# The order of the 256-column matmuls inside projection and output-projection tiles of a fused two-block transformer kernel

## The reference

```python
def memory_cross_attention(h, mem_n, w_cq, w_ck, w_cv, w_co):
    q = (h @ w_cq).reshape(bsz, seqlen, CROSS_HEADS, CROSS_HEAD_DIM)
    k = (mem_n @ w_ck).reshape(bsz, mlen, CROSS_HEADS, CROSS_HEAD_DIM)
    v = (mem_n @ w_cv).reshape(bsz, mlen, CROSS_HEADS, CROSS_HEAD_DIM)
    ...
    return o @ w_co

x = x + hybrid_mixer(rms_norm(x, norm_mix_w[l]), w_in_mix[l], ...)
x = x + memory_cross_attention(rms_norm(x, norm_cross_w[l]), rms_norm(mem, norm_mem_w[l]), ...)
```

## Time and profile before

| | |
|---|---|
| median of 3 runs | 1856.13 us |
| the profiled execution, its own time | 1856.43 us |
| its span, first to last instruction | 1854.6 us |
| TensorE matmuls, busy | 1839.3 us (99%), 12202 matmuls |
| TensorE weight loads, busy | 1657.6 us (89%), 12202 |
| VectorE | 1292.1 us (70%) |
| ScalarE | 968.9 us (52%) |
| GpSimd | 133.5 us (7%) |
| granted TensorE clock | 0.998, tenths 9 in all 40 slices |

### The profile page before, as it was taken

How to read it: one execution, slowest core, us unless ns; L and a number is a source line. 1 busy time by engine, 2 the same in 40 slices (tenths; PEclk the granted TensorE clock), 3 DMA queues, 4 the chain that set the end, 5 groups by cost and what they waited for, 6 DMA issues and landing times.

```text
span 1854.6 us, 29790 instructions
## 1 busy us (share of the span) xinstructions
PE 1839.3 (99%) x12202; PEld 1657.6 (89%) x12202; DVE 1292.1 (70%) x1499; ACT 968.9 (52%) x1329; POOL 133.5 (7%) x166
## 2 busy tenths in 40 slices
PE   9999999999999999999999999999999999999998
PEld 7888999899998888888899988888889969998887
DVE  7875687776567765776685777567758786467763
ACT  6654465565445554554454555455544575355542
POOL 1200000131010001000120100000000001010000
PEclk9999999999999999999999999999999999999999
DMA  7555454434435554555454455555554505435553
GB/s 289 212 204 182 160 174 156 149 127 169 159 132 204 187 190 174 208 191 191 159 182 154 165 187 198 184 184 197 186 192 175 199 10 193 160 119 211 185 201 113
DMA packets 45725, 325.15 MB, mean 175 GB/s; under 512 B 5293, under 2 KB 5429, under 8 KB 6560
## 3 DMA queue, kind: packets, MB, share of 16 engines
q1 hardware_dynamic: 44208, 316.56, 47.7%
q0 software_dynamic: 1248, 6.77, 1.1%
q10 hardware_dynamic: 144, 0.00, 0.0%
HBM read 322.26 MB, written 1.06 MB: 174 GB/s over the span
## 4 chain that ended last, share of the span: by engine, by line
PE 93%; DVE 5%; ACT 1%; issue 1%; POOL 0%; DMA 0%; POOLq 0%; DVEq 0%; SPq 0%; ACTq 0%
PE PS L688 25%; PE PS L747 13%; PE PS L691 13%; PE PS L561 9%; PE PS L562 9%; PE PS L563 9%; PE PS L749 6%; DVE w_lo L2082 1%; DVE xT L2105 1%; PE PS L799 1%; PE PS L781 1%; PE PS L1300 1%; PE PS L1339 1%; PE PS L1319 1%; ACT w_hi L1396 0%
## 5 line engine op out<-in xcount | busy, mean ns | idle before, releaser
L2082 DVE TENSOR_TENSOR w_lo<-raw,w_hi 128x2048 fp32r<-128x2048 f32 x295 | 679.0, 2304 | 261.6 <-ACT w_hi L1396 261.4
L688 PE MATMUL PS<-xT,w_hi 128*128 128x512 f32 x2096 | 732.0, 395 | 1.7 <-DVE arena L2244 1.5
L1396 ACT ACTIVATE w_hi<-raw 128x2048 fp32r<-128x2048 f32 x295 | 562.9, 1908 | 194.5 <-PE PS L563 143.7
L691 PE MATMUL PS<-xT,w_lo 128*128 128x256 f32 x2096 | 582.3, 278 | 0.0
L688 PEld LDWEIGHTS PS<-xT,w_hi 128*128 128x128 f32 x2096 | 393.2, 188 | 94.2 <-DVE arena L2244 1.8
L691 PEld LDWEIGHTS PS<-xT,w_lo 128*128 128x128 f32 x2096 | 394.0, 188 | 0.2
L561 PE MATMUL PS<-xT,w_hi 128*128 128x256 f32 x592 | 170.6, 288 | 0.5 <-DVE w_lo L2082 0.3
L747 PE MATMUL PS<-more_hidden,w_hi 128*128 128x512 f32 x480 | 169.6, 395 | 0.0
L562 PE MATMUL PS<-xT,w_hi 128*128 128x256 f32 x592 | 167.4, 283 | 0.0
L563 PE MATMUL PS<-xT,w_lo 128*128 128x256 f32 x592 | 167.4, 283 | 0.0
L747 PE MATMUL PS<-mT,w_hi 128*128 128x512 f32 x384 | 136.1, 395 | 0.0
(11 more groups left out here) (352 smaller groups left out, 3112.2 us busy)
## 6 DMA issues: line engine op xcount, KB each, us to landing
raw<-weights SPq DMA_DIRECT2D x299, 1024.0 KB, 4.8
arena<-mems POOLq DMA_DIRECT2D x5, 1024.0 KB, 5.1
x<-x_in SPq DMA_DIRECT2D x1, 1024.0 KB, 7.1
out<-x SPq DMA_DIRECT2D x4, 256.0 KB, 2.9
both<-toep POOLq DMA_DIRECT2D x1, 512.0 KB, 4.0
arena<-toep POOLq DMA_DIRECT2D x1, 512.0 KB, 4.5
con<-consts SPq DMA_DIRECT2D x1, 498.0 KB, 13.1
arena<-dtw SPq DMA_DIRECT2D x1, 256.0 KB, 13.5
```

Source lines behind the costliest of these rows:

```text
L688: pe.matmul(PS[:, bank + part, :], w_hi[:, slot, w:w + P], xT[:, k].rearrange("p a b -> p (a b)"), start=k == 0, stop=False, skip_group_ch ...
L691: last = pe.matmul(PS[:, bank + part, 0:S], w_lo[:, slot, w:w + P], xT_hi[:, k, :], start=False, stop=k == KC - 1, skip_group_check=True)
L1396: act.activation(w_hi[:, slot, :], raw[:, raw_slot, :], ACT.Copy).then_inc(hi_ready, 1)
L2082: dve.tensor_tensor(w_lo[:, slot, :], raw[:, raw_slot, :], w_hi[:, slot, :], ALU.subtract).then_inc(lo_ready, 1)
```

## The change

In `proj` the two halves of the output now run side by side: for each `k`, for each of the three products, one matmul into part 0 and one into part 1. In `accumulate` two chunks `d` run side by side in the same way, for each row chunk and product one matmul into each of the two. The number of matmuls, their shapes and their sums stay as they were (in tiles with `rows_out` the second and third product change places). `mid` and `mid2` fall after the same number of matmuls as before, 24 and 36. In a fresh tile there is now a wait before every `k`, each followed by 6 matmuls. In the last accumulate tile both waits for `x_ready` stand ahead of the pair, and both `chunk_done` come at its end.

```diff
-                for part, first in ((0, 0), (0, 4), (1, 0), (1, 4)) if fresh is None else ((0, 0), (1, 0), (0, 4), (1, 4)):
-                    for k in range(first, first + 4):
-                        if fresh is not None and part == 0:
-                            pe.wait_ge(split_done, fresh * KC + k + 1)
...
-                        last = mm3(o, a, b, c, d, k == 0 and (part == 0 or fresh is None), k == KC - 1)
+                for k in range(KC):
+                    if fresh is not None:
+                        pe.wait_ge(split_done, fresh * KC + k + 1)
+                    for product in range(3):
+                        for part in range(2):
+                            if rows_out:
+                                a = (hi, lo, hi)[product][:, k, part * P:(part + 1) * P]
+                                b = (w_hi, w_hi, w_lo)[product][:, slot, k * 256:(k + 1) * 256]
+                            else:
+                                w = k * 256 + part * P
+                                a = (w_hi, w_hi, w_lo)[product][:, slot, w:w + P]
+                                b = (hi, lo, hi)[product][:, k, :]
+                            last = pe.matmul(PS[:, bank, part * 256:(part + 1) * 256], a, b,
+                                             start=k == 0 and product == 0 and part == 0,
+                                             stop=k == KC - 1 and product == 2, skip_group_check=True)
...
-                for d in chunks:
-                    if stop and d >= 4:
-                        pe.wait_ge(x_ready, KC * (at.norm - 2) + d - 3)
+                for two in zip(chunks[0::2], chunks[1::2]):
+                    for d in two:
+                        if stop and d >= 4:
+                            pe.wait_ge(x_ready, KC * (at.norm - 2) + d - 3)
                     for k in range(2):
-                        w = k * D + d * P
-                        last = mm3(PS[:, d % 4, (d // 4) * S:(d // 4 + 1) * S],
-                                   w_hi[:, slot, w:w + P], w_lo[:, slot, w:w + P], right[:, k, 0, :], right[:, k, 1, :],
-                                   start and d < 4 and k == 0, stop and k == 1)
-                    if stop and d < KC - 1:
-                        last.then_inc(chunk_done, 1)
+                        for product in range(3):
+                            for d in two:
+                                w = k * D + d * P
+                                last = pe.matmul(PS[:, d % 4, (d // 4) * S:(d // 4 + 1) * S],
+                                                 (w_hi, w_hi, w_lo)[product][:, slot, w:w + P],
+                                                 right[:, k, product % 2, :],
...
+                                if stop and d < KC - 1 and k == 1 and product == 2:
+                                    last.then_inc(chunk_done, 1)
```

More of the change, by code:

```diff
@@ L617, in proj @@
                 pe.wait_ge(lo_ready, n + 1)
-                for part, first in ((0, 0), (0, 4), (1, 0), (1, 4)) if fresh is None else ((0, 0), (1, 0), (0, 4), (1, 4)):
-                    for k in range(first, first + 4):
-                        if fresh is not None and part == 0:
-                            pe.wait_ge(split_done, fresh * KC + k + 1)
[L622 to L630, removed]
-                        last = mm3(o, a, b, c, d, k == 0 and (part == 0 or fresh is None), k == KC - 1)
-                    if mid is not None and (part, first) == (0, 4):
+                for k in range(KC):
[13 more added lines that the diff above has]
+                                             stop=k == KC - 1 and product == 2, skip_group_check=True)
+                    if mid is not None and k == 3:
                         mid()
-                    if mid2 is not None and (part, first) == (1, 0):
+                    if mid2 is not None and k == 5:
                         mid2()
@@ L640, in accumulate @@
                 pe.wait_ge(lo_ready, n + 1)
-                for d in chunks:
-                    if stop and d >= 4:
-                        pe.wait_ge(x_ready, KC * (at.norm - 2) + d - 3)
+                for two in zip(chunks[0::2], chunks[1::2]):
+                    for d in two:
+                        if stop and d >= 4:
+                            pe.wait_ge(x_ready, KC * (at.norm - 2) + d - 3)
                     for k in range(2):
-                        w = k * D + d * P
-                        last = mm3(PS[:, d % 4, (d // 4) * S:(d // 4 + 1) * S],
-                                   w_hi[:, slot, w:w + P], w_lo[:, slot, w:w + P], right[:, k, 0, :], right[:, k, 1, :],
-                                   start and d < 4 and k == 0, stop and k == 1)
-                    if stop and d < KC - 1:
-                        last.then_inc(chunk_done, 1)
+                        for product in range(3):
[4 more added lines that the diff above has]
+                                                 right[:, k, product % 2, :],
+                                                 start=start and d < 4 and k == 0 and product == 0,
+                                                 stop=stop and k == 1 and product == 2, skip_group_check=True)
+                                if stop and d < KC - 1 and k == 1 and product == 2:
+                                    last.then_inc(chunk_done, 1)
                 if done:
```

## The result

| | before | changed |
|---|---|---|
| median of the runs, first set | 1856.1 us (6 runs) | 1858.9 us (6 runs, 1857.1 to 1864.4) |
| ratio, 95% interval | | 1.0024 [1.0013, 1.0034] |
| median, second set | 1856.5 us (35 runs, 1855.8 to 1857.9) | 1859.0 us (12 runs, 1853.7 to 1863.3) |
| ratio, 95% interval | | 1.0009 [0.9998, 1.0019] |
| profiled execution, its span | 1856.43, 1854.6 us | 1857.28, 1855.4 us |

The ratios are as the measurement gives them; the quotients of the medians are 1.0015 and 1.0013. The first interval lies above 1 and the second takes it in, so a slowdown of 0.1 to 0.2% is likely but not settled.

The account below looks back on a forecast made before the run. TensorE bounds the kernel, matmuls filling 99% of the span, with few waits for VectorE. From the profiled 1856.4, 0 + 0 + 1.9 gives 1858.3, less 0.3 to the runs' median: 1858.0 us, range 1842.5 to 1861.

Parts of the forecast that it names:

- Term 1: Reordered fp32r matmuls: alternating the place in PSUM leaves their 0.12 us spacing as it is, 0 us.
- A: Reordered matmuls: alternation helps in part, cost falls to 117 ns each, 15 us off, 1843; chance 12%.
- B: Reordered matmuls: alternation helps in full, 109 ns each, 50 us off, 1808; chance 8%.
- C: Reordered matmuls: adding into another place than the last costs 10 ns each, 45 us slower, 1903; chance 6%.
- Term 2: Other orders of products, stationary loads and x chunks in the changed tiles: no saved load lost, no new wait, 0 us.
- Term 3: Ends of five stages: later chunks delay VectorE's `w_lo` and TensorE's second tile, 3 x 0.42 + 2 x 0.30 = 1.9 us.
- Rival D: Stage ends cost more: whole 0.65 paid five times or pair (6, 7) stalls, 3.3 to 5 us; chance 13%.

## Why the prediction was right, and where it wasn't

The forecast was 1858.0 us in a range of 1842.5 to 1861, 63% for no measurable change. The median of the first set is 1858.9.

- **Term 1, the place in PSUM, 0: right.** 0.12 us a matmul in the changed tiles, nothing in the runs with the projections alone, 117 ns in the narrow ones either way. The reading that decided was the change of place after every sixth matmul. Rivals A, B and C are out.
- **Term 2, the other orders, 0: right.** No wait on the split appears in the fresh tiles, and none at the pair (6, 7): TensorE has no line for x's adds among its waits.
- **Term 3, the five ends, +1.9 us: right in sign and mechanism, too large.** Measured 1.1 us: 0.22 and 0.22 for the ends that a cross-attention follows where I had 0.30, and 0.25, 0.21 and 0.22 for those that a feed-forward follows where I had 0.42. I had GpSimd finish 4.04 us after the next stage's first matmul, as before; it finished at 547.14 - 543.22 = 3.92. `w_lo` then ended 2.49 behind it, as I had added up (0.3 + 2.15 to 2.29). So the error of the first figure is this 0.12. The second held one step more: I had chunk 7 at 4.41 after the stage's first matmul, and the matmul that needs it started at 4.26, so the stall was 0.37 where I had 0.58. Rival D, 3.3 us or more, is out.
- **What I had left out: the tiles that the change does not touch.** The prediction has "In the feed-forward tiles, six pairs take 602.66 - 600.58 = 2.08 us, 0.347 a pair". That was read at one place and taken for the price of a pair. A look at another stage of the same trace would have shown 0.353. The later ends that term 3 prices at 0.4 us also make the long streams run at one price in some executions and at the other in others, and that is worth some 3.4 us a stream. In the range I had stalls and not this; five of the 18 runs lie above its upper end. That the median came out close to 1858.0 is in part luck: no run took 1858.9 us, which is the middle between the third and fourth of six runs, 1857.28 and 1860.53, in two heaps. 1.1 us of it are the ends, the rest is runs that stand one or two steps up.
- **The 0.2%, 3.7 us, that a measurement was said to tell** was taken from a kernel whose runs agree. The first set gave 1.0024 with an interval to either side of 0.2%, the second 1.0009. Six runs with none in the lowest heap and twelve with four in it can differ so much by chance.

Shown: that alternation is free, that the last output tile carries the cost, that a price of 0.3467 or 0.3533 us a pair holds from one break to the next and is worth 3.2 us in one stage, and that a delay on VectorE alone, or one added matmul, makes the runs differ. Argued, and supported by profiles at 1853.9, 1857.3 and 1860.6 us: that all heaps are made of these two prices. Open: what on TensorE makes the two prices, and what picks one of them in a given run. All runs of the kernel before but three lie in one heap; why it is so steady was not found.

## What to carry to other kernels

Before two sums are laid side by side to spare TensorE the wait for its own last write, look for a place where the order changes the target already; here nothing gave there, and nothing gave when every matmul changed its target. A tile that hands its chunks over one by one is no place to pair chunks: it holds back every second one by half a pair, and the next engine's tail is what the next stage waits for. And when a change moves a median by less than 0.3%, list the runs: here heaps at a nearly fixed distance came from a stream with two speeds, and the count of matmuls in equal stretches found it.

## What the hardware showed beyond this

- A stream of pairs, 512 and 256 columns fp32r with a load each, ran at 346.7 or 353.3 ns a pair at the full granted clock, with TensorE never idle in either, and kept its price for up to 185 us. It changed only behind a break, once behind eight matmuls of one column at the same place in all thirteen profiles.
- A GpSimd sum of 0.74 us took 5.24 when VectorE had two `w_lo` in its queue.
- After 1.57 us of idle time on TensorE the granted clock fell to 0.50 at one of two like places, and the fall cost about as much again as the idle time.
